# Sample's softmax ahead of VectorE's last search, GpSimd's low halves inside its pooling groups, sample's own keys earlier on TensorE

## The reference, cut to what matters

```
h = rms_norm(x) * ln1;  u, q, k, v, qi, ki, wi, gates = split(h @ w_in)
branch A: for windows 2, 4, 8, 16 (one per group of 128 channels):
          a_pool = (mean over the window of u  -  u) @ pool_w[g] * pool_scale
branch B: score[t, s] = sum_h wi[t, h] * relu(qi[t, h] . ki[s]);  keep the 256 best keys s of each t
          a_attn = softmax(q.k + rel_bias over the kept keys) @ v
          (the 8 sample tokens do the same over 2048 cached keys and their own new key)
m = sigmoid(gates[:1024]) * (a_pool @ w_pool_proj) + sigmoid(gates[1024:]) * (a_attn @ w_attn_proj)
x1 = x + m @ w_out;  y = rms_norm(x1 + swiglu(rms_norm(x1)))
```

## Time and profile before

| what | us |
|---|---|
| median of 3 runs | 1576.95 |
| the profiled execution, its own time | 1577.05 |
| its span, first to last instruction | 1575.3 |
| TensorE busy in the span | 1508.5 (96%) |
| TensorE busy, 351 to 364 us | 0.19 of 13 |
| TensorE busy, 180 to 278 us | 90.4 of 98 |
| TensorE busy, 598 to 1575 us | 957.1 of 977 |
| VectorE, ScalarE, GpSimd busy in the span | 925.2, 561.9, 603.7 |

### The profile page before, as it was taken

One profiled execution on the slowest core, in us unless ns is written; L12 is line 12 of the kernel. 1 busy time (PEld: TensorE's weight loads), 2 busy tenths in 40 slices (PEclk: granted clock), 3 DMA queues, 4 the chain that ended last, 5 costly groups with the idle time before them and its releaser, 6 DMA issues.

```text
span 1575.3 us, 26180 instructions
## 1 busy us (share of the span) xinstructions
PE 1508.5 (96%) x9681; PEld 1393.6 (88%) x9681; DVE 925.2 (59%) x2173; ACT 561.9 (36%) x1131; POOL 603.7 (38%) x535
## 2 busy tenths in 40 slices
PE   6998998997999999999999999999999999999997
PEld 5873798667996678999998999999999999999997
DVE  5427985799966773233449655445555554555546
ACT  4324564322126664214235322422314224132233
POOL 4112294252444211111124643625537346264350
PEclk9999998998998999999999999999999999999999
DMA  6354111142200013220102210201102011021002
GB/s 219 110 174 185 35 28 29 50 152 94 55 27 2 1 42 101 74 67 29 41 27 81 81 55 27 80 21 59 53 27 80 27 53 53 27 80 53 27 6 116
DMA packets 101494, 100.30 MB, mean 64 GB/s; under 512 B 18278, under 2 KB 91638, under 8 KB 100893
## 3 DMA queue, kind: packets, MB, share of 16 engines
q1 hardware_dynamic: 93607, 88.14, 17.9%
q0 software_dynamic: 2688, 8.39, 1.7%
q10 hardware_dynamic: 5118, 2.69, 0.6%
HBM read 86.75 MB, written 12.68 MB: 63 GB/s over the span
## 4 chain that ended last, share of the span: by engine, by line
PE 58%; DVE 1%; POOL 1%; issue 1%; ACT 0%; POOLq 0%; DVEq 0%
PE banks L2068 28%; PE banks L2165 16%; PE banks L109 14%; DVE yo L2642 0%; PE banks L2025 0%; PE banks L2006 0%; PE banks L2182 0%; POOL wL L2216 0%; ACT XH L2284 0%; POOL hnL_lo L2229 0%; DVE hnL_hi L2497 0%; POOL dL L2213 0%; POOL T4L L2229 0%; ACT sH L2277 0%; ACT resid L2281 0%
## 5 line engine op out<-in xcount | busy, mean ns | idle before, releaser
L2216 POOL TENSOR_TENSOR wL<-w_raw,wH 128x512 fp32r<-128x512 f32 x176 | 231.2, 1328 | 315.1 <-ACT wH L2327 313.9
L2068 PE MATMUL banks<-hnH,wH 128*128 128x344 f32 x704 | 225.8, 321 | 2.1 <-POOL wL L2216 0.8
L2068 PE MATMUL banks<-hnH,wL 128*128 128x344 f32 x704 | 224.7, 319 | 0.0
L2629 DVE TENSOR_TENSOR resid<-resid,banks 128x344 f32<-128x344 f32 x264 | 132.1, 511 | 96.8 <-PE banks L2165 96.8
L2165 PE MATMUL banks<-aH,dH 128*128 128x344 f32 x528 | 169.3, 321 | 0.0
L2165 PE MATMUL banks<-aH,dL 128*128 128x344 f32 x528 | 169.1, 320 | 0.0
L2165 PE MATMUL banks<-aL,dH 128*128 128x344 f32 x528 | 168.2, 319 | 0.0
L1523 DVE TENSOR_SCALAR_CACHE_REDUCE pta<-SC,thr 128x512 uint8<-128x512 f32 (+4 forms) x160 | 144.0, 930 | 2.3 <-POOL SC L976 0.2
L2327 ACT ACTIVATE wH<-w_raw 128x512 fp32r<-128x512 f32 x176 | 109.6, 626 | 73.2 <-PE banks L2068 40.5
L2068 PEld LDWEIGHTS banks<-hnH,wH 128*128 128x128 f32 x704 | 132.1, 188 | 3.2 <-issue 1.9
L2068 PEld LDWEIGHTS banks<-hnH,wL 128*128 128x128 f32 x704 | 132.3, 188 | 0.0
(11 more groups left out here) (422 smaller groups left out, 3707.8 us busy)
## 6 DMA issues: line engine op xcount, KB each, us to landing
w_raw<-in_w_gate_up_dram SPq DMA_DIRECT2D x22, 1024.0 KB, 5.0
d_raw<-in_w_down_dram SPq DMA_DIRECT2D x11, 1024.0 KB, 4.9
big<-in_w_in_dram SPq DMA_DIRECT2D x11, 512.0 KB, 4.0
ZL<-x_lows SPq DMA_DIRECT2D x2, 2064.0 KB, 13.3
XL<-x_lows SPq DMA_DIRECT2D x2, 2064.0 KB, 8.1
W<-in_x_prompt_dram SPq DMA_DIRECT2D x8, 512.0 KB, 5.6
x_lows<-xnL SPq DMA_DIRECT2D x8, 512.0 KB, 3.6
slab_raw<-in_w_in_dram SPq DMA_DIRECT2D x8, 512.0 KB, 4.2
```

What stands on the lines that cost most here:

```text
L2068: last = mm(out, W_[w][s][:, i * P:(i + 1) * P], x_of(x)(i), start=start and i == 0 and j == 0, stop=stop and i == HALF - 1 and j == 2)
L2216: gp.tensor_tensor(wL[s].rearrange("p (k n) -> p k n", k=HALF), quadrant(x, *HOME[name]), f32(wH[s]).rearrange("p (k n) -> p k n", k=HALF) ...
L2629: V.tensor_tensor(resid[:, m, chunk(DOWN_ORDER[o])], resid[:, m, chunk(DOWN_ORDER[o])], ps[:, 4 + n % 4, 0:CH], ALU.add).then_inc(y_done, 1)
```

## The change: what it does

1. On VectorE the sample softmax moves up: it now stands behind the masks of blocks 2, 3 and 4. The mask of block 5 and all 32 rounds of blocks 6 and 7 come after it. On ScalarE `sample_exp` moves from before the evacuation of chunk 21 to before that of chunk 20.
2. On GpSimd the low halves of slabs 4 to 7 move: slab 4's to the end of group 1 (the same place in the stream), slab 5's from ahead of group 3 into group 2 before its long subtraction, slab 6's from behind group 3 into it, between its additions and its scaling, slab 7's stays last. The copy of the sample's column into `sx` and the wait for ScalarE's `stT_evac`, which in the first group stood ahead of everything, now stand behind the additions and the scaling of each group.
3. On TensorE the 16 one-column matmuls that multiply the sample's queries by their own new keys move from `begin_sample_logits` to behind `sum_lanes`.

```diff
-            ROUNDS_AHEAD = 5
@@ TensorE, behind the pooling products of group 1
                     if g == 1:
                         sum_lanes()
+                        own_key_logits()
@@ GpSimd
                 pool.wait_ge(sidx_used, NB)
-                pool.wait_ge(stT_evac, 1)
                 pool.wait_ge(pool_fill, 3)
                 for g in range(NG):
-                    if g >= 2:
-                        low_uq(g + 2)
                     pool.wait_ge(uq_evac, 3 * (g + 1))
-                    did(gp.tensor_copy(sx[:, g, :, POOLBUF], U[:, g, 16 + SEQ:16 + TOK]))
...
+                    if g == 3:
+                        low_uq(6)
                     sums = src[:, 16:16 + SEQ]
...
+                    if g == 0:
+                        pool.wait_ge(stT_evac, 1)
+                    did(gp.tensor_copy(sx[:, g, :, POOLBUF], U[:, g, 16 + SEQ:16 + TOK]))
...
+                    if g == 2:
+                        low_uq(5)
                     did(gp.tensor_tensor(Dp[:, g, 0:SEQ], Dp[:, g, 0:SEQ], U[:, g, 16:16 + SEQ], ALU.subtract))
...
+                    if g == 1:
+                        low_uq(4)
-                low_uq(6)
                 low_uq(7)
@@ ScalarE
-                    if x == 21:
+                    if x == 20:
                         sample_exp()
@@ VectorE
-                for k, i in enumerate((2, 3, 4, 5)):
+                for k, i in enumerate((2, 3, 4)):
                     to_mask(k, i)
-                dve.wait_ge(mask_ready, 4)
-                for r in range(ROUNDS_AHEAD):
-                    pair_round(slice(5, 7), (6, 7), r, rej_bank)
                 dve.wait_ge(sm_made, SM["S_ready"])
...
-                for r in range(ROUNDS_AHEAD, BITS):
+                to_mask(3, 5)
+                dve.wait_ge(mask_ready, 4)
+                for r in range(BITS):
                     pair_round(slice(5, 7), (6, 7), r, rej_bank)
```

More of the change, by code:

```diff
@@ L707, in _, with own_key_logits @@
                         transpose_last_u()
+                def own_key_logits():
+                    pe.wait_ge(lanes_made, 2)
+                    pe.wait_ge(zq_ready, 1)
+                    for j in range(2):
+                        for g in range(2):
+                            for rc in range(4):
+                                b = 4 * j + rc
+                                mm(ps[32 * rc:32 * rc + 32, 7, TOPK:TOPK + 1], ZQ[:, g, rc, j, :], kT[:, g, SEQ + b:SEQ + b + 1],
+                                   start=(j == 0 and g == 0), stop=(j == 1 and g == 1), tile_position=(0, 32 * rc))
                 def sum_lanes():
@@ L744, in begin_sample_logits @@
                     pe.wait_ge(sm_step, STEP["near"])
-                    pe.wait_ge(lanes_made, 2)
                     pe.wait_ge(table_made, 3)
-                    pe.wait_ge(zq_ready, 1)
                     mm(ps[:, 7, 384:385], row_of[:, :, :].rearrange("p rc n -> p (rc n)"), MK[:, P:P + 1], start=True, stop=True)
[L749 to L754, removed]
                     for j in range(2):
```

## The result

The changed kernel takes 1563.57 us (median of 4 runs, 1560.26 to 1564.1) against 1577.57 us for the kernel before, timed beside it (median of 4, 1576.63 to 1581.95): a ratio of 0.9901, 95% interval 0.9878 to 0.9925. That is faster by 14.0 us by the medians (15.6 by the ratio), where 22.6 were forecast. 1563.57 is 0.6 us above the upper end of the range, 1563; but the range was set on a before of 1576.95, and the one timed beside the change was 0.6 us slower, so the result stands at the very end of the range, and well outside the forecast's own 1551.5 to 1558. The profiled execution took 1564.1 us, its span 1562.4.

What follows compares the result with a forecast made beforehand. TensorE, busy 96% of the span, was taken as the bound, with idle time to recover before 598 us. 12.4 + 10.5 - 0.3 = 22.6 us off 1577.05 gave 1554.5 us; range 1551 to 1563, forecast's own 1551.5 to 1558.

Steps and rivals of the forecast that it cites:

- Part A: GpSimd's low halves inside the pooling groups end TensorE's waits in the q slabs: 12.4 us, bounds 4.3 and 12.4.
- The search: VectorE's search, needed by TensorE at 264.9, loses 9.4 us of waits for ScalarE's counts and ends at 260.9.
- Rival 1: VectorE's search becomes the wait of the q slabs; Part A gives only 4.3 us: 1562.6 us, chance 0.10.
- Own keys: 16 one-column matmuls moved within TensorE's stream: value 0, bounds -0.5 and +0.5 us.
- Part B: Softmax ahead of the rounds removes TensorE's 13.16 us wait; 10.5 of 14.7 us gained reach the row minima.
- the forecast's 1.7: Block 5's mask on VectorE meets the first gate slab's low half on GpSimd and loses 1.7 us.
- rival 3: The gates bound after all: row minima wait for GpSimd's last product, 456.8 in place of 461.0; 1550.3 us, chance 0.04.
- rival 2: All of Part B is given back: blocks 6 and 7's search takes 0.33 us more per round; 1565.0 us, chance 0.08.
- 10.5 forecast: Gain at VectorE's first row minimum from Part B: 461.0 in place of 471.50, bounds 14 and 8 us.
- the sum had 15.2: VectorE's masks of blocks 6 and 7 behind the rounds: 17.1 us, less 1.9 us of waiting for GpSimd.
- The 0.3 us for the longer pause ahead of the attention: TensorE's pause grows by some 4 us; slow clock in the attention's first blocks then costs 0.3, between nothing and 1.5.
- three things that would make it wrong: TensorE waits over 1 us at either changed place, a round is not 2.78 us, or row minima wait for GpSimd.

Runs made afterwards that it cites:

- changed kernel with plain fetches: Changed kernel with the 16 gathers of keys replaced by plain transfers of the same size from fixed rows: 1554.97 us, ratio 0.9852.
- all gathers spaced: Changed kernel with two small GpSimd operations after every second gather of keys and behind each pair of value gathers: 1558.96 us, ratio 0.9874.
- first trace of before: The kernel before the change, unaltered, in the trace from which the forecast was made: 1577.57 us timed beside the change.
- before with plain fetches: Kernel before the change with the 16 gathers of keys replaced by plain transfers from fixed rows: 1575.30 us, ratio 0.9994.
- before again: The kernel before the change, unaltered, run once more for a second trace: 1579.82 us.
- softmax part alone: Kernel before with only the VectorE and ScalarE edits (softmax ahead of the last mask and rounds, exponential one chunk earlier): 1581.19 us, ratio 1.0009; with plain key transfers 1564.75 us.
- GpSimd part alone: Changed kernel with VectorE's and ScalarE's order as before, low halves and own keys still moved: 1566.69 us, ratio 0.9917; with plain key transfers 1564.11 us.
- in fours: GpSimd waits for the landing after every fourth key gather: on the changed kernel 1566.56 us, on the softmax part alone 1578.42 us.
- key gathers spaced: Changed kernel with two small GpSimd operations after every second gather of keys, value gathers as they were: 1560.52 us, ratio 0.9896.

## Why the prediction was right or wrong

**Part A, right.** 12.4 us forecast, ties' matmul at 264.9: it ran at 265.06. The low halves are 0.1, 0, 0.4 and 0.1 us from their forecast places. The search was in time, done at 261.6 (forecast 260.9): VectorE waits 4.14 us for TensorE there, at the first instruction behind the ties' matmul. Its waits for ScalarE's counts fell from 11.2 us to 2.3 (forecast near 2). Rival 1 is refuted.

**Own keys, right.** 0.43 us for all of them at 269.62, with no wait.

**Part B, right in its working, read without the standstill.** In the changed kernel with plain fetches the exponential starts right behind its table load, and the late rows of VectorE stand where the forecast had put them (last round about 433, first row minimum 448.6, VectorE busy up to it):

```profile
331.25 1.28 ACT L1311 ACT_TABLE_LOAD   x1
332.54 0.48 ACT L1311 ACTIVATE I<-banks,W 128x257 f32<-128x257 f32 x1
```
```profile
337.39 2.26 DVE L1518 TENSOR_SCALAR pta<-SC,thr 128x768 bf16<-128x768 f32 x1
...
432.75 0.17 DVE L1508 TENSOR_SCALAR thr<-thr 128x2 f32<-128x2 f32 x1
...
448.83 0.28 DVE L1741 CUSTOM_DVE_ANT_0 W<-banks,small 128x128 f32<-128x128 f32 x1
```

The row at 337.39 is block 5's mask in the grip of GpSimd's first low half, which started at 336.88: 2.26 us, where the same instruction on the same columns took 0.63 alone in the version with all gathers spaced (338.26). That is 1.6 us for the forecast's 1.7, with GpSimd the first to start. By the rule of the Trainium skill that I had cited ("SBUF — State Buffer", "Who interferes with whom") the order of starting decides, and the trace agrees. 32 rounds took 2.78 us each (354.00 to 443.00 in the changed kernel). The gates' end was no bound (rival 3), and the search gave nothing back (rival 2). What was a little high is the gain between ties and row minimum: 10.5 forecast, 193.7 - 184.7 = 9.0 measured with plain fetches (9.5 from the first trace of before). 0.9 of it are the late masks, 16.1 us from 432.75 to the first row minimum where the sum had 15.2. The 0.3 us for the longer pause ahead of the attention can't be seen: from the first row minimum to the end of the span it is 1102.5 us, and 1101.3 and 1103.8 in before with plain fetches and in its first trace.

**The step that failed** is the sentence ahead of part B, "I keep the old times and subtract 12.4 at the end", that is, that everything between the ties and the softmax stays as the one trace showed it. It stood in the trace, and it was one of two courses that this stretch takes. The prediction gave the stretch no term and no rival. With the standstill the changed kernel has 194.0 us between ties and row minimum, without it 184.7: 9.3 us. By the ratios, 0.9901 and 0.9910 against 0.9852, it costs 8 to 9 us. 22.6 less 9 is 13.6; 14.0 were measured. How late it makes TensorE at the probabilities, counted from the ties' matmul, and how much of that reaches the first row minimum:

| kernel | TensorE late by | seen at the row minimum |
|---|---|---|
| before again | 14.7 | 3.0 |
| softmax part alone | 15.0 | 15.0 |
| GpSimd part alone | 10.0 | 4.2 |
| changed | 9.4 | 9.3 |

The reference is the first trace of before for the first row and the same kernel with plain fetches for the others (73.2 to 73.5 us). Where a wait for VectorE follows, it pays 11.7 us in before and 5.8 in the GpSimd part alone; where the softmax part has taken that wait away, all is seen. That also explains why the softmax part alone measured nothing: it is worth 11.7 us and uncovers 12 more of the standstill than before shows.

My rival 2 gave 1565.0 and the time came out near it, for another reason: the softmax was not given back in the search. And the range reached up to 1563 for the sake of rival 1, which did not happen either, so that the result stands at its end by luck. The prediction had named three things that would make it wrong, and none of them came: they all watched the places of the change, and the loss stands between them. The times forecast behind it gave it away, such as the first row minimum at 448.6, which came at 459.09.

**What stays open.** Why engines stop while gathers follow one another without a break, and why before escaped it in one trace of two with all 32 gathers in an unbroken row. Shown is: it was in none of the four traces with plain key fetches, it moved when the unbroken row moved (in fours, key gathers spaced), and it was gone but for the two remnants in the one trace where no row was left (all spaced). Since before can escape by chance, one trace is weak evidence each; for the changed kernel the times back it, 1553.1 to 1555.5 us in four runs with plain fetches against 1560.3 to 1569.5 in eight with gathers. Not shown is what carries it. The bytes are not the cause: it comes at a DMA share of 0.32 to 0.35, and before ran undisturbed at 0.48.

A rival that no run here tests is the recording itself. Every execution timed here lists a granted clock, so each was recorded, and the records get thin where the engines stand: of the 256 landings that the 16 key gathers report, the first trace of before holds 248 and before again 50, the changed kernel 55, every kernel with plain fetches all 256. An engine that has to stop until its record is written would also stop inside a chunk and behind its own instructions, and missing records may be what makes a wait "remote". Against it as the whole story: with all gathers spaced only 148 of the 256 are recorded, and next to nothing stands. Whether an execution that is not recorded has the standstill, and so whether the change is worth 14 us there or some 22, is open.

## What to carry to other kernels

Trace the kernel before more than once before building on the times of a stretch: a disturbance that a wait absorbs hardly shows in the median (3 us of 1577 here), and is paid in full by the change that removes the wait. When a change brings less than its sum, look first for a wait at a place that it does not touch. And read "remote" releasers, or an engine waiting for itself, as a sign that no engine is slow: then look for what is in flight, and for whether the recording keeps up.

## What the runs showed of the hardware that was not expected

- Beside a row of row-by-row gathers on GpSimd's queue, 1.25 us apart, engines of the core can stand for 7 to 19 us by ScalarE's longest gap, in recorded executions. At 3.1 us for a pair two signals in the time of 32 gathers came 1.5 and 2 us late, no more. Beside 16 plain transfers of the same size, issued in 8.7 us, nothing stood.
- The Trainium skill, page "SBUF — State Buffer", section "Who interferes with whom", says that TensorE and ScalarE never wait on anyone. No run here tests that for the ports. Both engines stood here while gathers ran, ScalarE for 10.8 us; whether what held them is a port or something else is not shown.
- Some gathers took longer to issue while VectorE made its masks: 1.4 to 1.9 us instead of 0.95 in the last version. No run takes the masks away, so that VectorE is the cause is not shown.
